# Merging two matmul passes into one of 512 columns in a single-core transformer kernel, with the halves added on VectorE

## The reference, cut to what matters

```python
proj = u @ w_in                                   # u: normed activations, 2048 features
y = y @ w_out
h = jnp.square(jax.nn.relu(u @ w1)) @ w2          # w1 2048 x 8192, w2 8192 x 2048, twice
q = apply_rope((u @ w_q)...)                      # then causal_diff_attention, then o @ w_o
```

## Time and profile before

| what | value |
|---|---|
| median of 3 runs | 3623.08 us |
| lowest and highest run | 3620.05 and 3623.44 us |
| span of the profiled execution | 3620.8 us |
| own time of the profiled execution | none is given apart from its span |
| PE busy, PEld busy | 3553.3 us (98%), 3463.1 us (96%) |
| DVE, ACT, POOL busy | 1912.4 us (53%), 1482.7 us (41%), 182.7 us (5%) |
| DMA, mean rate | 165 GB/s |

### The profile page before, as it was taken

How to read it: one execution, slowest core, us unless ns; L and a number is a source line. 1 busy time by engine, 2 the same in 40 slices (tenths; PEclk the granted TensorE clock), 3 DMA queues, 4 the chain that set the end, 5 groups by cost and what they waited for, 6 DMA issues and landing times.

```text
span 3620.8 us, 64661 instructions
## 1 busy us (share of the span) xinstructions
PE 3553.3 (98%) x28024; PEld 3463.1 (96%) x28024; DVE 1912.4 (53%) x1661; ACT 1482.7 (41%) x1475; POOL 182.7 (5%) x178
## 2 busy tenths in 40 slices
PE   7999999999999999999999999999999999999998
PEld 7898889999999999999999999999988999999998
DVE  6644445555554665555444444554576554545454
ACT  4334334333334457544333333343345443434342
POOL 1140000000000012010000000010000100000001
PEclk9999999999999999999999999999999999999999
DMA  6543334455556544555555555555542665656564
GB/s 192 176 134 105 110 112 140 140 185 185 185 186 186 185 148 135 175 175 173 173 174 173 174 174 174 174 174 163 175 128 95 186 186 186 186 186 186 186 186 140
DMA packets 578814, 597.73 MB, mean 165 GB/s; under 512 B 11712, under 2 KB 565952, under 8 KB 578656
## 3 DMA queue, kind: packets, MB, share of 16 engines
q1 hardware_dynamic: 574752, 588.42, 52.0%
q0 software_dynamic: 1408, 5.39, 0.5%
q10 hardware_dynamic: 2496, 1.56, 0.2%
HBM read 593.23 MB, written 2.10 MB: 164 GB/s over the span
## 4 chain that ended last, share of the span: by engine, by line
PE 92%; DVE 4%; ACT 1%; DMA 1%; issue 1%; SPq 0%; POOL 0%; ACTq 0%; DVEq 0%; POOLq 0%
PE acc L484 27%; PE acc L486 27%; PE acc L485 27%; PE psx L848 1%; DVE low L1434 1%; PE psx L687 1%; PE psx L712 1%; ACT high L995 1%; PE acc L831 1%; PE psx L831 1%; PE psx L833 1%; PE acc L833 1%; PE acc L832 1%; PE psx L832 1%; DMA raw<-in_w_in 1%
## 5 line engine op out<-in xcount | busy, mean ns | idle before, releaser
L484 PE MATMUL acc<-gh,high 128*128 128x256 f32 (+1 forms) x5440 | 1574.3, 289 | 25.7 <-DVE low L1434 20.0
L486 PE MATMUL acc<-gh,low 128*128 128x256 f32 (+1 forms) x5440 | 1555.4, 286 | 0.0
L485 PE MATMUL acc<-gl,high 128*128 128x256 f32 (+1 forms) x5440 | 1551.8, 285 | 0.0
L1686 DVE TENSOR_TENSOR low<-raw,high 128x2048 fp32r<-128x2048 f32 x374 | 857.1, 2292 | 597.5 <-ACT high L1173 597.5
L484 PEld LDWEIGHTS acc<-gh,high 128*128 128x128 f32 x5440 | 1037.1, 191 | 39.7 <-issue 29.8
L485 PEld LDWEIGHTS acc<-gl,high 128*128 128x128 f32 x5440 | 1038.0, 191 | 3.0 <-issue 2.0
L486 PEld LDWEIGHTS acc<-gh,low 128*128 128x128 f32 x5440 | 1037.0, 191 | 0.0
L1173 ACT ACTIVATE high<-raw 128x2048 fp32r<-128x2048 f32 x374 | 714.5, 1911 | 662.6 <-DMA raw<-in_mlp_w 518.2
L1434 DVE TENSOR_TENSOR low<-raw,high 128x2048 fp32r<-128x2048 f32 x180 | 418.7, 2331 | 314.8 <-ACT high L995 314.3
L486 PE MATMUL acc<-fh,low 128*128 128x272 f32 (+1 forms) x2048 | 584.5, 285 | 0.0
L484 PE MATMUL acc<-fh,high 128*128 128x272 f32 (+1 forms) x2048 | 583.2, 285 | 0.0
(11 more groups left out here) (338 smaller groups left out, 3253.2 us busy)
## 6 DMA issues: line engine op xcount, KB each, us to landing
raw<-in_mlp_w SPq DMA_DIRECT2D x256, 1024.0 KB, 5.6
raw<-in_w_in SPq DMA_DIRECT2D x60, 1024.0 KB, 5.3
raw<-in_a_w_in SPq DMA_DIRECT2D x40, 1024.0 KB, 5.1
raw<-in_w_expert_gate SPq DMA_DIRECT2D x32, 1024.0 KB, 5.3
raw<-in_w_expert_up SPq DMA_DIRECT2D x32, 1024.0 KB, 5.3
raw<-in_w_expert_down SPq DMA_DIRECT2D x32, 1024.0 KB, 5.6
raw<-in_w_kv SPq DMA_DIRECT2D x32, 1024.0 KB, 5.4
raw<-in_a_w_out SPq DMA_DIRECT2D x20, 1024.0 KB, 5.1
```

The costliest lines, as they stand in the source:

```text
L484: pe.matmul(o, hw[:, k, c], h, start=first, stop=False)
L485: pe.matmul(o, hw[:, k, c], l, start=False, stop=False)
L486: m = pe.matmul(o, lw[:, k, c], h, start=False, stop=last)
L1686: dve.tensor_tensor(low[:, k % SLOTS, :], raw[:, k % SLOTS, :], high[:, k % SLOTS, :].bitcast(F32), ALU.subtract)\
```

## The change

In every stage of 256 tokens the rounded activations and their rests now lie side by side in one buffer (`g1`, `g2`, `g6`, `g7`, `pp`, `yy`, `oo`, `hid`, `ff`, of shape tiles x 2 x 256). One matmul of 512 columns takes both against the high weights, and a second of 256 columns adds low times rounded onto the second half. The output of a tile now fills a whole PSUM bank: the first half holds high times rounded, the second half the two corrections. VectorE adds the halves when it takes a pair: `fold` is a new tensor_reduce over the two halves ahead of the operation that was there, `add_halves` adds them to the residual in two operations where there was one, and in wpool two more small operations follow the first two. The stages of 272 tokens keep their three matmuls. Buffers are laid out anew, so that the joined ones fit.

```diff
-            def unit(u, slot, half, nhalf, pair, rh, rl, mid=None, free=None, need=None):
+            def both(x):
+                return lambda kt: x[:, kt, :, :]
+
+            def unit(u, slot, half, nhalf, pair, x, xl=None, mid=None, free=None, need=None):
...
+                        if xl is None:
+                            o = acc[:, 2 * (pair % 2) + n, :]
+                            pe.matmul(o, hw[:, k, c], x(kt).rearrange("p a t -> p (a t)"), start=first, stop=False)
+                            m = pe.matmul(o[:, S:2 * S], lw[:, k, c], x(kt)[:, 0, :], start=False, stop=last)
+                            continue
+                        h, l = x(kt), xl(kt)
+                        o = acc[:, 2 * (pair % 2) + n, 0:h.shape[-1]]
                         pe.matmul(o, hw[:, k, c], h, start=first, stop=False)
                         pe.matmul(o, hw[:, k, c], l, start=False, stop=False)
                         m = pe.matmul(o, lw[:, k, c], h, start=False, stop=last)
...
-            def take_pair(b, to):
-                m = dve.tensor_tensor(to, acc[:, 2 * (b % 2):2 * (b % 2) + 2, 0:S], over2(inv[:, 0:S]), ALU.mult)
-                return m
+            def fold(b, n, to, i=0):
+                dve.tensor_reduce(to, acc[:, 2 * (b % 2):2 * (b % 2) + 2, :].rearrange("p n (a t) -> p n t a", a=2),
+                                  AX.X, ALU.add).then_inc(folded, 1)
+                dve.wait_ge(folded, i * 2 + (n + 1))
+
+            def add_halves(b, n, h, i=0):
+                s = acc[:, 2 * (b % 2):2 * (b % 2) + 2, :]
+                dve.tensor_tensor(h, h, s[:, :, S:2 * S], ALU.add).then_inc(folded, 1)
+                dve.wait_ge(folded, i * 2 + (n + 1))
+                dve.tensor_tensor(h, h, s[:, :, 0:S], ALU.add).then_inc(acc_free, 1)
+
+            def take_pair(b, n, to):
+                fold(b, n, to)
+                return dve.tensor_tensor(to, to, over2(inv[:, 0:S]), ALU.mult)
...
-                        m = dve.tensor_scalar(pb[:, t, :], acc[:, 2 * (b % 2) + k, 0:S], col("pool_scale", t), None, ALU.mult)
+                        m = dve.tensor_scalar(pb[:, t, :], acc[:, 2 * (b % 2) + k, S:2 * S], col("pool_scale", t), None, ALU.mult)
+                    link(m)
+                    for k in range(2):
+                        t = 4 * POOL_ORDER[2 * j + q // 2] + 2 * (q % 2) + k
+                        m = dve.scalar_tensor_tensor(pb[:, t, :], acc[:, 2 * (b % 2) + k, 0:S], col("pool_scale", t),
+                                                     pb[:, t, :], ALU.mult, ALU.add)
...
-                        dve.tensor_tensor(h, h, acc[:, 2 * (b % 2):2 * (b % 2) + 2, 0:T], ALU.add).then_inc(acc_free, 1)
+                        if T == S:
+                            add_halves(b, F0[name] + b_off + pr, h, i)
...
-                            dve.scalar_tensor_tensor(z, acc[:, 2 * (b % 2):2 * (b % 2) + 2, 0:T], 0.0, over2(inv[:, 0:T]),
-                                                     ALU.max, ALU.mult).then_inc(acc_free, 1)
+                            src = acc[:, 2 * (b % 2):2 * (b % 2) + 2, 0:T]
+                            if T == S:
+                                src = z
+                                fold(b, F0[name] + 16 * c + pr, z, i)
+                            dve.scalar_tensor_tensor(z, src, 0.0, over2(inv[:, 0:T]), ALU.max, ALU.mult).then_inc(acc_free, 1)
...
                 src = acc[:, 2 * (b % 2):2 * (b % 2) + 2, tok]
-                T = tok.stop - tok.start
+                if T == S:
+                    fold(b, F0["q"] + t, to)
+                    src = to
```

More of the change, by code:

```diff
@@ L65 @@
           ("mlp0", 128, 64), ("v", 16, 8), ("k", 16, 8), ("q", 16, 8), ("o", 16, 8), ("mlp1", 128, 64)]
-U0, B0 = {}, {}
-_u = _b = 0
+WIDE = ("wpool", "a_in", "a_out", "mlp0", "v", "k")
+U0, B0, F0 = {}, {}, {}
+_u = _b = _f = 0
 for _n, _c, _p in STREAM:
-    U0[_n], B0[_n] = _u, _b
-    _u, _b = _u + _c, _b + _p
+    U0[_n], B0[_n], F0[_n] = _u, _b, _f
+    _u, _b, _f = _u + _c, _b + _p, _f + (0 if _n in WIDE else _p)
 NUNITS = _u
@@ L222, in mixer_moe_rnn_attention @@
         pw, _ = at("pw", [P, 3, 2, S], w_wh)
[L223 to L226, removed]
+        pp, w = at("pp", [P, 8, 2, S], w_ym, F32R)
+        yy, w = at("yy", [P, KT, 2, S], WORK, F32R)
         GA, GB = WORK, WORK + 2 * KT * TB
         HID = GB + 2 * KT * TB
[L230 to L235, removed]
+        g2, w = at("g2", [P, KT, 2, S], HID, F32R)
+        hid, w = at("hid", [P, 2 * NEXP, 2, S], GA, F32R)
+        weight, w = at("weight", [P, 2 * NEXP, 2, S], GA)
+        assert w <= HID
+        SQ0 = HID + 2 * KT * TB + 64
+        sq, w = at("sq", [P, 2, 2, TB], SQ0)
         SQ_END = w
@@ L280, in mixer_moe_rnn_attention @@
         gsub, w = at("gsub", [P, 2], w)
[L281 to L284, removed]
+        oo, w = at("oo", [P, KT, 2, S], GA, F32R)
+        g7, w = at("g7", [P, KT, 2, S], GB, F32R)
         result, w = at("result", [P, KT, S], GA)
+        gh1, gl1, gh2, gl2, gh6, gl6, gh7, gl7 = (x[:, :, j, :] for x in (g1, g2, g6, g7) for j in range(2))
+        ph, pl, yh, yl, oh, ol, hidh, hidl = (x[:, :, j, :] for x in (pp, yy, oo, hid) for j in range(2))
+        fsh, fsl = (ff[:, :, j, :] for j in range(2))
         acc = ctx.enter_context(nc.psum_tensor("acc", [P, 4, 512], F32))
@@ L754, in need_y @@
                     pe.wait_ge(y_lo, kt // 2 + 1)
-            pairs_stage("wout", 8, 2, lambda kt: yh[:, kt, :], lambda kt: yl[:, kt, :], first=need_y,
+            pairs_stage("wout", 8, 2, both(yy), None, first=need_y,
                         mid=lambda: heads_out(NKV - 1))
@@ L817, in need_hid @@
                 return need
-            pairs_stage("down", 8, 4, lambda kt: hidh[:, kt, :], lambda kt: hidl[:, kt, :], first=need_hid(0))
+            pairs_stage("down", 8, 4, both(hid), None, first=need_hid(0))
             def out_tiles(u, slot, h, l, lo_kt, nkt, banks, first, last):
@@ L1421, in _ @@
                 body(i)
-            mlp("mlp1", 5, S, NEXP + 32, (6, 2, 7, None, None, TOK), last=True)
+            mlp("mlp1", 5, S, NEXP + 32, (6, 2, 7, None, None, TOK), fsh, last=True)
             root(6, S)
@@ L1765, in _ @@
             m.then_inc(comb_done, 1)
-            even = weight[:, :, :].rearrange("p (e two) t -> p e two t", two=2)[:, :, 0, :]
+            even = weight[:, :, 1, :].rearrange("p (e two) t -> p e two t", two=2)[:, :, 0, :]
             def take_weights(n):
@@ L1789, in expert @@
                     dve.wait_ge(wt_out, 1)
-                wt = weight[:, ds(i * 2, 1), :].to_broadcast([P, 2, S])
-                dve.tensor_tensor(zb[:, 1, :, 0:S], src, wt, ALU.mult).then_inc(acc_free, 1)
+                wt = weight[:, ds(i * 2, 1), 1, :].to_broadcast([P, 2, S])
+                fold(b, F0["experts"] + 1, zb[:, 1, :, 0:S], i)
+                dve.tensor_tensor(zb[:, 1, :, 0:S], zb[:, 1, :, 0:S], wt, ALU.mult).then_inc(acc_free, 1)
                 dve.wait_ge(silu_e, i + 1)
@@ L2080, in _ @@
                 body(i)
-            mlp("mlp1", 5, S, NEXP + 32, (7, None, None, None, TOK, TOK), last=True)
+            mlp("mlp1", 5, S, NEXP + 32, (7, None, None, None, TOK, TOK), fsh, fsl, last=True)
             root(6, S)
```

76 lines of the change are left out of this document (38 added, 38 removed).

## The result

The changed kernel takes 3637.65 us, the median of 7 runs (3627.89 to 3648.51), against 3621.8 us for the kernel before beside it: a ratio of 1.0051, 95% interval 1.0035 to 1.0067. It is slower by half a per cent, where 3595 us had been forecast. Ratios here are of medians over runs on one chip. Runs of one kernel lie 5 to 25 us apart, so the profiled executions (3620.8 us before, 3646.7 us after) serve for places and durations, and the medians for sums.

What follows compares the result with a forecast made beforehand. TensorE's matmul count and pace were taken to bound the kernel, outside a few seams. From 3620.8 us, 55 us saved on TensorE and 29 us lost to VectorE gave 3595 us; the 8-in-10 range was 3545 to 3648 us.

Steps and rivals of the forecast that it cites:

- X: Time of one merged 512-column matmul on TensorE until the next starts; forecast 224.5 ns.
- 55 us: TensorE's forecast saving in 256-token stages: 11.3 ns times 5344 products, 60 us, less what does not arrive.
- Rival 2: TensorE's surplus belongs to the columns, X = 233.3 ns; 13 us saved, VectorE's 29 us decide: 3637 us; chance 0.22.
- Rival 1: The long 512-column stream hides TensorE's whole surplus, X = 215.8 ns: 3552 us; chance 0.22.
- VectorE's term: VectorE's folds and second additions where not hidden, in q, wpool, qkv and pool, merge and stage ends: 29 us lost.
- q from 15: In the q stage the fold ahead of the rotation delays the next period: 8 x 1.89 = 15 us.
- wpool, 7.7 us for 5: In wpool each of 8 takings gets two more operations; 3 us hidden by matmuls, 5 us lost.
- qkv and pool: 14 folds, 26 us, come in front of low halves and head norms; gaps take most, 4 us lost (0 to 12).
- Merge's 2 us: At the seam from merge to wout, 2 us lost, up to 8 if the softmax is held up.
- 3 us for the last additions: Second additions ahead of a norm at the ends of wout, down, o and mlp1: 4 x 0.7 = 3 us.
- its own test: The prediction counts as wrong if the 512-column matmul's time in mlp1, forecast 224 ns, is off by more than 4 ns.
- second sign: The prediction counts as wrong if TensorE waits for VectorE in merge, experts or mlp1 at all.

Runs made afterwards that it cites:

- two half changes: The changed kernel with TensorE's part undone (3644.17 us, ratio to before 1.0066), and with VectorE's part undone, leaving out the corrections (3612.41 us, 0.9984).
- experiment 2: The changed kernel with only TensorE's part undone, 3644.17 us, then with only VectorE's part undone, 3612.41 us; ratios to before 1.0066 and 0.9984.
- experiment 1: Separate kernel computing nothing of the reference: rows of 96 matmuls by type and width; float32r 226.7 ns at 512 columns, 120.0 at 256; bf16 215.8 and 109.2.
- grouped kernel: The changed kernel reordered: eight 512-column matmuls of an output tile in a row, then eight of 256; 3611.03 us, ratio 0.9955 to before.
- half change: For VectorE's cost: the changed kernel with VectorE's folds and second additions undone and the corrections left unread; 3612.41 us, ratio 0.9984 to before.
- second profile: The changed kernel run again unaltered and profiled once more; 3640.7 us, ratio 1.0039 to before.
- onehalf: The changed kernel with VectorE's part undone, TensorE's matmuls as changed, corrections computed but not read; 3612.41 us, ratio 0.9984 to before.
- seams: The changed kernel with qkv, pool, wpool, merge and q put back as before, the long stages kept merged; 3617.57 us, ratio 0.9988 to before.

## Why the prediction was wrong, step by step

- **What bounds the kernel** was right: TensorE's pace and a few seams.
- **The step that failed** is "I take the surplus as one per matmul, X = 213.3 + 11.2 = 224.5 ns". In the changed kernel X is 233.6 and its neighbour of 256 columns rose from 117.8 to 119.7, so a product kept its 353 ns. Where the step had 55 us, the changed kernel's long stages save 1 us by pace, in o, against the same kernel with three matmuls. The two half changes give 6 us (0 to 11), but through mlp1 at a pace that the changed kernel does not have (experiment 2). The reasoning left out that the pace of float32r matmuls depends on which matmuls follow each other. The rule "one surplus per matmul" holds in rows of one form (experiment 1) and was carried to a row of two forms, where 346.7 and 353.3 both occur. One of my facts pointed there, the 113.3 ns of the earlier trace rows: I read it as a load and a stream that meet well or badly, and then took one number for the meeting all the same. It should have widened the chances of X at both ends, not supported the middle.
- **Rival 2** named the time, 3637 us with X = 233.3, but by luck and for a wrong reason. It had 13 us saved and 29 us lost to VectorE, and both were less. The surplus does not belong to the columns: 13.3 ns at 256 and 13.4 at 512 alone, and 229.0 ns in the grouped kernel. Its X was right because 353.3 ns per product is nearly what a proportional cost gives too (353.7). **Rival 1** (X = 215.8, whole surplus hidden) is reached by bf16 only, and by no float32r row.
- **VectorE's term** was right in kind and too high in sum: 29 us forecast, 24 (18 to 30) by the half change, 17 and 24 by the two profiles. The fold was mis-sized: 1.84 taken, 1.22 us measured, the in-line reduction of the earlier trace rows; inputs 1 KB apart in PSUM cost no more than inputs in line. That lowers q from 15 to 9.3 us in the trace, with the mechanism and place as described. It was partly offset by wpool, 7.7 us for 5: the wait grew until the granted clock fell to 0.50 behind it, a price that the step lacked. qkv and pool with 4.9 (3.9 in the second profile) for 4 fit. Merge's 2 us are not shown, as its rows overlap with and without the fold. Of the 3 us for the last additions the wait for `yy` shows 1.2. In the long stages the folds are hidden, as said.
- **DMA** stayed covered, with no wait of its own among TensorE's large ones.
- **What would show it:** X off by 9 ns made the forecast wrong by its own test. The second sign came too, in small: in merge TensorE waited four times for VectorE's `probs`, 0.8 us in all, where it had not waited before, and 5.2 us for ScalarE's `pts`. Inside experts and mlp1 it waited for VectorE not at all.

**What stays open:** what decides the rhythm in a given stage (mlp1 of the changed kernel at 353.3, of onehalf and seams at 348.9 with the same matmuls), why three matmuls of 256 run at 353 in the kernels and at 360 alone, and why the grouped order runs at 345 in the kernel and at 349 alone. The runs show that the start can decide it for 512 and 256 in turn, and that VectorE, ScalarE and DMA don't do so by their load; the mechanism inside TensorE was not found.

## What to carry to other kernels

Count merged matmuls by the pace of the row they will stand in, not by the surplus of one: measure the exact sequence of widths, and the same sequence in another order, before laying out buffers for it. If a saving of a few ns per matmul is bought with work on another engine, keep the change to the stages where that engine's result is wanted late; here five of ten stages carried nearly all of the loss. And a wait that grows can cost the clock behind it as well.

## What the hardware showed that I had not expected

- A row of 512- and 256-column float32r matmuls in turn runs at 346.7 or at 353.3 ns per product, each kept over 12 to 71 products; grouped by eight it ran at 349.2 alone and 345 in the kernel.
- float32r has 11.7 to 13.4 ns on top of the array's time in long rows, bf16 2.5 (215.8 and 109.2 ns), and zeros or half the rows change nothing (226.7 for both).
- A reduction over pairs 1 KB apart in PSUM takes as long as one over neighbours: 1224 ns for 1024 inputs, against 1225 in the earlier trace rows. The 1.80 ns per input of the SBUF reduction there was no guide for PSUM. The Trainium skill, VectorE: DVE Perf Modes, Rules for kernel authors, has tensor_reduce in the slowest mode only; with that mode taken as one input per cycle at 0.96 GHz the fold would be about 1.1 us (an estimate from that page), and the trace is 15% over it.
- After 4.69 us without work TensorE ran at a granted clock of 0.50, 640 ns for a product; in the kernel before, the longest wait of wpool, 2.6 us, left it at 1.00 (stretch 243 to 259 us). The length of that one wait does not decide it: after 2.32 us in the changed kernel the clock was 0.50 too.
